# Two more slice pairs of each head pair as seven products of quarters, with work moved from VectorE to ScalarE

## The chip, the cores and the metric

The kernel runs on one core of one Trainium2 chip, as one launch. The metric is the device time of the whole program in microseconds (us), the median of several runs. All arithmetic is float32.

## The reference, cut to what matters

Two model blocks follow each other over 256 tokens of width 1024. The first projects the normed input with one wide matrix, and feeds four branches of 8 heads: a state-space scan (a), a block attention (b), a forgetting attention (c) and a sliding-window attention (d). The change lies in that projection.

```python
proj = h @ w_in
(m_z, m_xbc, m_dt, b_qkv, c_qkv, c_f, d_q, d_kv, gate_logits) = jnp.split(proj, SPLIT_POINTS, axis=-1)
y_a = mamba2_branch(m_z, m_xbc, m_dt, ...)          # x and z of the state: parts of m_xbc and m_z
y_b = moba_attention(heads(bq), heads(bk), heads(bv), ...)
y_c = forgetting_attention(heads(cq), heads(ck), heads(cv), c_f + forget_bias)
y_d = sliding_window_attention(heads(d_q), heads(dk), heads(dv), ...)
branch_out = jnp.einsum('bsiw,iwd->bsid', branches, w_branch)
gates = jax.nn.sigmoid(gate_logits)
x = x + jnp.sum(gates * branch_out, axis=2) @ w_out
```

## The kernel before, in words

The program is written out by hand for each engine: an engine runs its own list of instructions in order, and a step waits on counters of the steps that it needs. What is named `steps` in the code (`pe.step("g5734.0.1")`) is such a count. Nothing is reordered by a scheduler.

The first block does its heads in four **head pairs** (`pe_heads`, `act_heads`, `dve_heads`, `sp_heads`, i = 0 to 3). Each pair takes 17 slices of the wide matrix, each 128 columns by 1024 rows, loaded by SyncE into twelve 512 KB `slots`: q, k and v of b and c (BQ, BK, BV, CQ, CK, CV), q of d (DQ), the state's x and z (XS, ZS), and eight gate slices. A slice's product with the 256 tokens is plain (`project`: 8 matmuls of 128x256), or two slices together are done as **seven products of quarters**: tokens halved, rows halved, the two slices as the two column halves, seven products of four 128x128 matmuls (`quarter_product`) in place of eight. For this VectorE first makes sums of the weight quarters (s3, s1, s2, s4: four operations on 128x512, s1 in place in the slot), and afterwards puts the results together (a first sum, and three others, L2018 and L2025 to L2029 for gates). In the kernel before the gates (`gate_pair`, four a pair) and q and k of b and of c (`qk_pair`, in pairs 1 to 3) go this way; the values of b and c (L677, one matmul over two slices) and x and z (L491) are plain.

The order on TensorE in a pair: q/k of b, of c, q of d, the scores (L569), the values, x, z, the turning of the first head's softmax weights (L575 to L577), gate_pair(0), the turning of x (L700, L701) and of the second head's weights, gate_pair(1), the weighing of the values (L595, L597), gate_pair(2), and in pair 3 a sum of squares (`ya.sum`), gate_pair(3).

VectorE interleaves with this the maxima of the scores (L1954), the softmax weights (L1967), the convolution of x (L1869, L1873, L1876), the sums for the gates (`slice_sums`, L2006 to L2012; `first_sums`; `other_sums`), and `ada(0)` to `ada(5)` (L1983), six steps a pair that gather a modulation for the second block from 512 KB loads into two buffers.

SyncE issues all loads of a pair in one order, and waits before each until its buffer is free. The part that matters here, for pair i:

```python
ada_load(2)
...
ada_load(3)      # waits for ada(1)
gate_load(3)
...              # BV and CV of pair i + 1, gate_load(6)
ada_load(4)      # waits for ada(2): two buffers
gate_load(7)
decay_loads(i + 1)
gate_load(4)     # slots 9 and 10, free when gate_pair(0) is done
gate_load(5)
ada_load(5)      # waits for ada(3)
```

gate_load(4) and gate_load(5) bring the slices of gate_pair(2), gate_load(2) and gate_load(3) those of gate_pair(1). `decay_loads` are two broadcast loads of 384 and 256 KB, not there in pair 3.

Of the kernel before, what the change touches and what calls it, by code (L numbers as in the profile page):

```python
# [147 lines left out]
def build(nc, a, out):  # L148

    with ExitStack() as ctx:  # L150
# [106 lines left out]
        vs = carve(TT, 2 * P)  # L257
# [6 lines left out]
        xsT = carve(T)  # L264
        xdt = carve(TT, P)
        zs = carve(T)
# [151 lines left out]
        S["d1"] = bank[1][:, T:T + P], bank[0][:, T:]  # L418
# [3 lines left out]
        QK_SLOTS = {"b": (BQ, BK), "c": (CQ, CK)}  # L422
# [32 lines left out]
        def qk_banks(i):  # L455

            return [view3(bank[(i + n) % 2][:, :], P) for n in range(2)]
# [121 lines left out]
        def weigh_two(e, i, one, two):  # L579

            def parts(what, hh):
                if what == "y":
                    return xdt[:, 0, hh * HD:hh * HD + HD], xdt[:, 1, hh * HD:hh * HD + HD], dec[hh]
                if what == "d":
                    g = hh * HD
                    return dv[:, 0, g:g + HD], dv[:, 1, g:g + HD], PT[hh][2]
                at = "bc".index(what) * P + hh * HD
                return vs[:, 0, at:at + HD], vs[:, 1, at:at + HD], PT[hh]["bc".index(what)]
# [11 lines left out]
        def pe_heads(e, i):  # L600
            def gate_pair(n):
# [24 lines left out]
            def qk_pair(b):  # L626

                even, odd = QK_SLOTS[b]
                one, two = qk_banks(i)
                s2, s3, s4 = gate_sums(i - 1, "bc".index(b))  # L630
                low, high = hT[:, 0:4, :], hT[:, 4:8, :]
                e.wait_ge(*in_slot[even].upto(f"w{even}.{i}"))
                e.wait_ge(*dve.upto(f"gc11.3.{i - 1}" if b == "b" else f"qk11.b.{i}"))
                quarter_product(e, one[:, 0, :], slot[even][:, 0:512], low[:, :, tokens(0)])
                quarter_product(e, one[:, 1, :], slot[even][:, 512:], high[:, :, tokens(0)])
                e.wait_ge(*dve.upto(f"qs2.{b}.{i}"))
                quarter_product(e, one[:, 2, :], s2, xt[1]).then_inc(*pe.step(f"q126.{b}.{i}"))
                e.wait_ge(*dve.upto(f"gc1221.3.{i - 1}" if b == "b" else f"qk1221.b.{i}"))
                e.wait_ge(*dve.upto(f"qs4.{b}.{i}"))
                quarter_product(e, two[:, 0, :], slot[odd][:, 0:512], xt[0])  # L640
                quarter_product(e, two[:, 1, :], s3, xt[2])
                quarter_product(e, two[:, 2, :], s4, high[:, :, tokens(1)])
                quarter_product(e, two[:, 3, :], slot[odd][:, 512:], xt[3]).then_inc(*pe.step(f"q5734.{b}.{i}"))

            if i:
                qk_pair("b")
                qk_pair("c")
# [22 lines left out]
            e.wait_ge(*dve.upto(f"qd.{i}"))  # L670
            scores(e, "d", i).then_inc(*pe.step(f"s.d.{i}"))

            e.wait_ge(*in_slot[BV].upto(f"w{BV}.{i}"))
            e.wait_ge(*in_slot[CV].upto(f"w{CV}.{i}"))
# [6 lines left out]
            e.wait_ge(*in_slot[XS].upto(f"w{XS}.{i}"))  # L681
            e.wait_ge(*dve.upto(f"mx.d11.{i}"))
            project(e, part(i, 5), slot[XS], hT).then_inc(*pe.step(f"xs.{i}"))
            e.wait_ge(*in_slot[ZS].upto(f"w{ZS}.{i}"))
            project(e, part(i, 6), slot[ZS], hT).then_inc(*pe.step(f"zs.{i}"))

            e.wait_ge(*dve.upto(f"v.{i}"))
# [14 lines left out]
            e.wait_ge(*dve.upto(f"p.b1.1.{i}"))  # L702
            e.wait_ge(*act.upto(f"pt.b0.{i}"))
            turn_weights(e, "b", 1).then_inc(*pe.step(f"t.b1.{i}"))
            e.wait_ge(*dve.upto(f"p.c1.1.{i}"))
            e.wait_ge(*dve.upto(f"pt.c0.{i}"))
            turn_weights(e, "c", 1).then_inc(*pe.step(f"t.c1.{i}"))
            e.wait_ge(*dve.upto(f"p.d1.1.{i}"))
# [5 lines left out]
            e.wait_ge(*dve.upto(f"pt.c1.{i}"))  # L714
# [143 lines left out]
        def quarter_product(e, out, w, rhs):  # L858
            for k in range(4):
                end = e.matmul(out, w[:, k * P:(k + 1) * P], rhs[:, k, :], start=k == 0, stop=k == 3)  # L860
            return end
# [618 lines left out]
        def act_heads(e, i):  # L1480
# [9 lines left out]

            def exps(b):
# [27 lines left out]
            for b in "bcd":  # L1519
                exps(b)  # L1520
            e.wait_ge(*pe.upto(f"xs.{i}"))
            e.wait_ge(*dve.upto(f"xs.tap3.{i - 1}" if i else "bc3.tap3"))
            e.activation(pad1[:, CONV1 - 1:], part(i, 5), ACT.Copy).then_inc(*act.step(f"xpad.{i}"))
            e.wait_ge(*pe.upto(f"zs.{i}"))
            if i:
                e.wait_ge(*dve.upto(f"zs.{i - 1}"))
            e.activation(zt, part(i, 6), ACT.Tanh, scale=0.5).then_inc(*act.step(f"zt.{i}"))
            e.wait_ge(*dve.upto(f"xs.tap3.{i}"))
            e.activation(th[:, :], conv[:, :], ACT.Tanh).then_inc(*act.step(f"xs.tanh.{i}"))
            turned("b", 0)  # L1530
            turned("d", 0)
# [5 lines left out]
            turned("b", 1)  # L1537
            turned("d", 1)
# [393 lines left out]
        def dve_heads(e, i):  # L1932
# [25 lines left out]
            def weights(hh):  # L1958
# [3 lines left out]
                e.wait_ge(*dve.upto(f"r.{hh}.{i}"))  # L1962
                for n, b in enumerate("bcd"):
                    for t in range(TT):
                        at, m = (0, P) if t == 0 else (P + 1, T)
                        w = Lg[hh][:, n, at:at + m]
                        e.tensor_scalar(w, w, sm[:, 6 * hh + 2 * n + t:6 * hh + 2 * n + t + 1], None,  # L1967
                                        ALU.mult).then_inc(*dve.step(f"p.{b}{hh}.{t}.{i}"))

            def turned(hh):  # L1970
                e.wait_ge(*pe.upto(f"t.c{hh}.{i}"))
                if i:
                    e.wait_ge(*pe.upto(f"pv.c0b1.{i - 1}"))
                e.tensor_copy(PT[hh][1], TURN["c"][:, 0:3 * P]).then_inc(*dve.step(f"pt.c{hh}.{i}"))
# [19 lines left out]
            def slice_sums(n):  # L1994

                even, odd = GATE_SLOTS[n]
                s2, s3, s4 = gate_sums(i, n)
# [5 lines left out]
                elif i:  # L2003
                    e.wait_ge(*pe.upto(f"q5734.c.{i}"))
                    e.wait_ge(*dve.upto(f"mx.d11.{i - 1}"))
# [25 lines left out]
            def qk_sums(b, i):  # L2031

                even, odd = QK_SLOTS[b]
                s2, s3, s4 = gate_sums(i - 1, "bc".index(b))
# [3 lines left out]
                e.wait_ge(*pe.upto(f"g5734.{2 if b == 'b' else 3}.{i - 1}"))  # L2038
# [8 lines left out]
            def qk_first(b):  # L2047

                q = qk[b]
                e.wait_ge(*act.upto(f"qp1.{b}.{i}"))  # L2050
                e.tensor_tensor(q[:, 0:4:3, :], q[:, 1:2, :].to_broadcast([P, 2, P]), qk_banks(i)[0][:, 1:3, :],
                                ALU.add).then_inc(*dve.step(f"qk11.{b}.{i}"))

            def qk_other(b):

                q, two = qk[b], qk_banks(i)[1]
# [8 lines left out]
            if i:  # L2065
                qk_sums("c", i)
                qk_first("b")
                ada(0)
                qk_other("b")
# [1360 lines left out]
```

## Time and profile before

| what | value |
|---|---|
| median of 3 runs | 1058.26 us (1057.3 to 1058.48) |
| the profiled execution | 1057.9 us |
| its span, first to last instruction | 1055.9 us |
| TensorE busy | 1045.8 us (99%) |
| VectorE busy | 754.8 us (71%) |
| ScalarE busy | 237.4 us (22%) |
| moved by DMA | 162.67 MB, mean 154 GB/s |

The span is shorter than the profiled execution by what lies before the first and after the last instruction. A float32 matmul stands in the trace as two records, so a quarter product is 8 records and seven of them 56. A busy TensorE is an engine with a matmul in flight.

### The profile page before, as it was taken

What the parts mean: (1) busy time and instruction counts of PE and PEld (TensorE: products, weight loads), DVE (VectorE), ACT (ScalarE), POOL (GpSimd) and SP (SyncE); (2) the same over time, 40 slices, a digit from 0 to 9 for tenths busy, and PEclk for the clock granted to TensorE, in tenths of its full rate; (3) what the DMA queues carried; (4) which work ended last, traced back from release to release, by engine and by line L of the source; (5) the groups of instructions that cost most, each with busy time, mean ns of one, the idle gap of its engine ahead of it and who ended that gap; (6) DMA issues with size and microseconds to landing.
All of it is one profiled execution on the core that took longest, in us unless ns stands there. A gap on an engine that the chain in (4) does not pass through costs nothing.

```text
span 1055.9 us, 21666 instructions
## 1 busy us (share of the span) xinstructions
PE 1045.8 (99%) x8902; PEld 904.3 (86%) x8902; DVE 754.8 (71%) x1714; ACT 237.4 (22%) x630; POOL 121.0 (11%) x166
## 2 busy tenths in 40 slices
PE   9999999999999999999999999999999999999997
PEld 8899899998988499999644988898898989887983
DVE  4488776867743477777757788767878778777875
ACT  4032222213300120011101432323223232324101
POOL 1101000000045121100250000000000000000052
PEclk9999999999999999999999999999999999999999
DMA  8786666552377446554555333333333322161261
GB/s 271 260 308 234 208 197 220 194 186 86 120 228 230 159 71 251 195 190 162 182 194 220 99 102 101 99 103 101 105 102 97 120 82 80 42 241 41 81 160 40
DMA packets 72307, 162.67 MB, mean 154 GB/s; under 512 B 18929, under 2 KB 33169, under 8 KB 72210
## 3 DMA queue, kind: packets, MB, share of 16 engines
q1 hardware_dynamic: 71202, 159.67, 46.1%
q8 instruction: 71, 1.16, 0.4%
q10 hardware_dynamic: 1008, 1.63, 0.4%
q14 instruction: 26, 0.21, 0.1%
HBM read 160.17 MB, written 1.11 MB: 153 GB/s over the span
## 4 chain that ended last, share of the span: by engine, by line
PE 97%; DVE 1%; DMA 1%; issue 0%; ACT 0%; POOL 0%; DVEq 0%; ACTq 0%; POOLq 0%
PE bank L860 27%; PE bank L1015 18%; PE bank L491 13%; PE bank L926 6%; PE bank L1041 4%; PE bank L677 3%; PE bank L792 2%; PE bank L835 2%; PE bank L1186 2%; PE bank L1198 2%; PE bank L1355 2%; PE bank L988 1%; PE bank L1077 1%; PE bank L994 1%; PE bank L569 1%; PE bank L1055 1%
## 5 line engine op out<-in xcount | busy, mean ns | idle before, releaser
L1015 PE MATMUL bank<-hT,slots 128*128 128x256 f32 x896 | 204.5, 382 | 0.0
L1015 PEld LDWEIGHTS bank<-hT,slots 128*128 128x128 f32 x896 | 167.8, 190 | 23.2 <-issue 0.3
L860 PE MATMUL bank<-hT,slots 128*128 128x128 f32 x832 | 103.5, 276 | 0.0
L2511 DVE SCALAR_TENSOR_TENSOR arena<-padA,par,arena 128x256 f32<-128x256 f32 x232 | 102.8, 504 | 0.0
L860 PEld LDWEIGHTS bank<-hT,slots 128*128 128x128 f32 x832 | 97.9, 192 | 0.8 <-issue 0.7
L860 PE MATMUL bank<-arena,slots 128*128 128x128 f32 x768 | 95.6, 275 | 0.0
L860 PEld LDWEIGHTS bank<-arena,slots 128*128 128x128 f32 x768 | 90.9, 192 | 0.5
L491 PE MATMUL bank<-hT,slots 128*128 128x256 f32 x336 | 74.4, 380 | 0.0
L491 PEld LDWEIGHTS bank<-hT,slots 128*128 128x128 f32 x336 | 63.4, 190 | 9.2 <-issue 0.8
L491 PE MATMUL bank<-arena,slots 128*128 128x256 f32 x304 | 66.3, 380 | 0.5 <-DMA slots<-in_w_br 0.5
L491 PEld LDWEIGHTS bank<-arena,slots 128*128 128x128 f32 x304 | 57.5, 190 | 8.8 <-DMA slots<-in_w_br 1.1
L926 PE MATMUL bank<-slots,arena 128*128 128x512 f32 x128 | 55.4, 592 | 0.0
L926 PEld LDWEIGHTS bank<-slots,arena 128*128 128x128 f32 x128 | 24.2, 190 | 30.1 <-issue 25.6
L3052 POOL TENSOR_TENSOR arena<-arena 128x256 f32<-128x256 f32 x8 | 5.8, 728 | 359.8 <-ACT arena L1726 359.8
L860 PE MATMUL bank<-x,arena 128*128 128x128 f32 x352 | 46.5, 275 | 0.0
L860 PE MATMUL bank<-x,slots 128*128 128x128 f32 x352 | 46.5, 275 | 0.0
L860 PEld LDWEIGHTS bank<-x,slots 128*128 128x128 f32 x352 | 42.8, 192 | 0.0
L860 PEld LDWEIGHTS bank<-x,arena 128*128 128x128 f32 x352 | 42.8, 192 | 0.0
L1983 DVE SCALAR_TENSOR_TENSOR adaA<-arena,sc,adaA 128x1024 f32<-128x1024 f32 x24 | 30.7, 1277 | 0.0
L1595 ACT ACTIVATE arena<-bank 128x128 f32<-128x128 f32 x20 | 5.5, 277 | 110.2 <-PE bank L860 98.9
L2981 POOL TENSOR_TENSOR arena<-arena 128x256 f32<-128x256 f32 x8 | 8.0, 1020 | 188.8 <-DMA arena<-cum_scratch 188.8
L2168 DVE SCALAR_TENSOR_TENSOR arena<-arena,bank 128x256 f32<-128x256 f32 x32 | 12.6, 415 | 22.9 <-PE bank L491 15.8
(478 smaller groups left out, 1887.5 us busy)
## 6 DMA issues: line engine op xcount, KB each, us to landing
slots<-in_w_rwkv SPq DMA_DIRECT2D x72, 512.0 KB, 3.6
slots<-in_w_heads SPq DMA_DIRECT2D x64, 512.0 KB, 4.5
slots<-in_w_gu SPq DMA_DIRECT2D x44, 512.0 KB, 4.5
arena<-in_ada_w SPq DMA_DIRECT2D x24, 512.0 KB, 5.5
slots<-in_w_down SPq DMA_DIRECT2D x20, 512.0 KB, 4.4
slots<-in_w_br SPq DMA_DIRECT2D x32, 256.0 KB, 2.8
slots<-in_w_out SPq DMA_DIRECT2D x16, 512.0 KB, 4.2
slots<-in_w_y SPq DMA_DIRECT2D x16, 512.0 KB, 6.5
```

The source lines that it names most:

```text
L491: end = e.matmul(psum, w[:, k * P:(k + 1) * P], rhs[:, k, :], start=k == 0, stop=k == kt - 1)
L677: end = e.matmul(view3(bank[5][:, t * T:(t + 1) * T], P), hT[:, k, t * P:(t + 1) * P], slots[:, BV:CV + 1, k * P:(k + 1) * P], start=k == ...
L792: return e.matmul(bank[DOWN_BANK[m]][:, :], *sides, start=j == 0, stop=j == OUT_PAIRS - 1)
L835: end = e.matmul(psum[:, tokens(t)], w[:, k * P:(k + 1) * P], hT[:, k, tokens(t)], start=k == 0, stop=k == KT - 1)
L860: end = e.matmul(out, w[:, k * P:(k + 1) * P], rhs[:, k, :], start=k == 0, stop=k == 3)
L926: return e.matmul(bank[DOWN_BANK[m]][:, :], *sides, start=j == 0, stop=j == DOWN - 1)
L1015: end = e.matmul(proj(w, q), slot[w][:, k * P:(k + 1) * P], hT[:, k, :], start=k == 0, stop=k == KT - 1)
L1041: end = e.matmul(out[:, at, :], w[:, k * P:(k + 1) * P], rhs[:, k, :], start=k == 0, stop=k == 3)
L1186: end = e.matmul(bank[2][r, c * CHUNK:(c + 1) * CHUNK], Nt[r, c, :], Xs[r, c, :], start=True, stop=True)
L1198: end = e.matmul(chunks(half(3))[r, c, :], Z[r, c, :], Gs[r, c, :], start=True, stop=True)
L1983: e.scalar_tensor_tensor(out=third, in0=adaW[n % 2], scalar=sc[:, 2 * i + n // 3:2 * i + n // 3 + 1], in1=third, op0=ALU.mult, op1=ALU.add ...
L2511: e.scalar_tensor_tensor(out=o, in0=src, scalar=w, in1=o, op0=ALU.mult, op1=ALU.add).then_inc(*dve.step(f"tap{n}.{q}"))
```

## The change

In every head pair the values of b with those of c (called "v"), and x with z ("z"), are done as seven products of quarters by `slice_pair`, which was `qk_pair`. For the values the roles in the matmul are turned (`quarter_product_turned`: tokens stand, weights move), since tokens are wanted on the rows. VectorE makes eight more weight sums a pair (`pair_weights`) and puts two more results together (`pair_first`, `pair_other`). The copy of the values out of PSUM falls away. The second head's softmax weights are scaled by ScalarE (`second_weights`), as are q of d; the turned weights of c are copied by ScalarE. The places of `slice_sums` and `ada` in VectorE's list move. SyncE's list keeps its order; the steps that its waits name change.

```diff
             def slice_pair(b):
+                even, odd = PAIR_SLOTS[b]
+                one, two = pair_banks(b, i)
+                s2, s3, s4 = pair_sums(b, i)
+                product = quarter_product_turned if b == "v" else quarter_product
...
+                elif b == "z":
+                    e.wait_ge(*dve.upto(f"qk11.v.{i}"))
+                product(e, one[:, 0, :], slot[even][:, 0:512], low[:, :, tokens(0)])
+                product(e, one[:, 1, :], slot[even][:, 512:], high[:, :, tokens(0)])
+                e.wait_ge(*dve.upto(f"qs2.{b}.{i}"))
+                product(e, one[:, 2, :], s2, xt[1]).then_inc(*pe.step(f"q126.{b}.{i}"))
...
+                product(e, two[:, 3, :], slot[odd][:, 512:], xt[3]).then_inc(*pe.step(f"q5734.{b}.{i}"))
@@ pe_heads
-            for t in range(TT):
-                for k in range(KT):
-                    end = e.matmul(view3(bank[5][:, t * T:(t + 1) * T], P), hT[:, k, t * P:(t + 1) * P],
-                                   slots[:, BV:CV + 1, k * P:(k + 1) * P], start=k == 0, stop=k == KT - 1)
-            end.then_inc(*pe.step(f"vbc.{i}"))
-            project(e, part(i, 5), slot[XS], hT).then_inc(*pe.step(f"xs.{i}"))
-            project(e, part(i, 6), slot[ZS], hT).then_inc(*pe.step(f"zs.{i}"))
+            slice_pair("v")
+            slice_pair("z")
@@ act_heads
+            def second_weights():
+                e.wait_ge(*dve.upto(f"r.1.{i}"))
+                for n, b in enumerate("bcd"):
+                    for t in range(TT):
...
+                        e.activation(w, w, ACT.Copy, scale=sm[:, 6 + 2 * n + t:6 + 2 * n + t + 1]).then_inc(*act.step(f"p.{b}1.{t}.{i}"))
...
+            exps("b")
+            exps("c")
+            pair_product("v")
+            exps("d")
+            second_weights()
...
+            pair_product("z")
+            e.wait_ge(*dve.upto(f"qk1221.z.{i}"))
+            e.activation(pad1[:, CONV1 - 1:], xsT, ACT.Copy).then_inc(*act.step(f"xpad.{i}"))
+            e.activation(zt, zs, ACT.Tanh, scale=0.5).then_inc(*act.step(f"zt.{i}"))
+            turned("b", 0)
+            turned("c", 0)
+            turned("d", 0)
             e.wait_ge(*dve.upto(f"xs.tap3.{i}"))
             e.activation(th[:, :], conv[:, :], ACT.Tanh).then_inc(*act.step(f"xs.tanh.{i}"))
@@ dve_heads
             for b in "bcd":
                 maxima(b)
+            pair_first("v")
             decays(0)
             decays(1)
-            slice_sums(1 if i else 0)
-            if i == 0:
-                ada(0)
-            e.tensor_copy(vs, view3(bank[5][:, :], T)).then_inc(*dve.step(f"v.{i}"))
-            weights(0)
-            ada(2 if i else 1)
+            pair_other("v")
+            inverses(0)
+            first_weights()
+            inverses(1)
+            slice_sums(0)
+            pair_first("z")
             if i == 0:
                 ada(0)
+            pair_other("z")
             conv_silu(e, ("xs", f".{i}"), act.upto(f"xpad.{i}"), i * CONV1, 8 * CONV1 + i, xsT)
...
-            weights(1)
-            turned(0)
             if i == 0:
-                ada(2)
-                slice_sums(1)
+                ada(1)
             first_sums(0)
-            ada(3)
+            slice_sums(1)
             other_sums(0)
+            ada(2)
             e.wait_ge(*pe.upto(f"turn.x.{i}"))
...
-            turned(1)
-            ada(4)
+            ada(3)
             first_sums(1)
             slice_sums(2)
             other_sums(1)
+            ada(4)
             slice_sums(3)
```

**How it moves instructions.** TensorE, head pair 1, from the last score matmul on; L677 is the values, L491 x and z:

```order
L569 MATMUL bank0<-arena 128x256
L677 MATMUL bank5<-slots,hT 128x256 x16
L491 MATMUL bank1<-hT,slots 128x256 x8
L491 MATMUL bank0<-hT,slots 128x256 x8
L575 MATMUL bank5<-cst,arena 128x128
```

The same place in the changed kernel; L870 is the turned quarter product, L865 the other, L580 the first turning of weights:

```order
L574 MATMUL bank5<-arena 128x256
L870 MATMUL bank1<-slots,hT 128x128 x8
L870 MATMUL bank1<-arena,x 128x128 x4
L870 MATMUL bank0<-slots,x 128x128 x4
L870 MATMUL bank0<-arena,x 128x128 x4
L870 MATMUL bank0<-arena,hT 128x128 x4
L870 MATMUL bank0<-slots,x 128x128 x4
L865 MATMUL bank1<-hT,slots 128x128 x8
L865 MATMUL bank1<-x,arena 128x128 x4
L865 MATMUL bank0<-x,slots 128x128 x4
L580 MATMUL bank5<-cst,arena 128x128
```

Thirty-two matmuls of 128x256 have become 56 of 128x128.

VectorE, head pair 1, before, from `ada(2)` (the first L1983) to `other_sums(0)`; L1869 to L1876 are the convolution, L1974 the copy of turned weights, L2018 `first_sums(0)`:

```order
L1983 SCALAR_TENSOR_TENSOR adaA<-arena,sc,adaA 128x1024
L1869 TENSOR_SCALAR conv<-padA,arena 128x256
L1873 SCALAR_TENSOR_TENSOR conv<-padA,arena,conv 128x256 x3
L1876 SCALAR_TENSOR_TENSOR arena<-th,conv 128x256
L2096 SCALAR_TENSOR_TENSOR arena<-arena,bank1 128x256
...
L1974 COPY arena<-bank2 128x384
L2018 TENSOR_TENSOR arena<-arena,bank0 128x2x128
L1983 SCALAR_TENSOR_TENSOR adaA<-arena,sc,adaA 128x1024
L2025 TENSOR_TENSOR arena<-arena,bank1 128x256
```

The same stretch in the changed kernel; L1905 ends the convolution, L2043 is `first_sums(0)`, L2031 to L2037 `slice_sums(1)`, L2050 to L2054 `other_sums(0)`, L2007 `ada(2)`:

```order
L1905 SCALAR_TENSOR_TENSOR arena<-th,conv 128x256
L2126 SCALAR_TENSOR_TENSOR arena<-arena 128x256
L2043 TENSOR_TENSOR arena<-arena,bank0 128x2x128
L2031 TENSOR_TENSOR arena<-slots 128x512
L2033 TENSOR_TENSOR slots<-slots 128x512
L2035 TENSOR_TENSOR arena<-slots 128x512
L2037 TENSOR_TENSOR arena<-slots,arena 128x512
L2050 TENSOR_TENSOR arena<-arena,bank1 128x256
L2052 TENSOR_TENSOR arena<-arena,bank1 128x128
L2054 TENSOR_TENSOR arena<-arena,bank1 128x256
L2007 SCALAR_TENSOR_TENSOR adaA<-arena,sc,adaA 128x1024
```

`ada(2)`, which stood ahead of the convolution, now stands behind `slice_sums(1)` and `other_sums(0)`.

## Rows read from the trace of the kernel before

**Rows 1.** The waits of TensorE over the whole span: us, times, longest.

```profile
PE bank L522 <- POOL padA L2972: 1.2, 1, 1.2
...
PE bank L491 <- DMA slots<-in_w_br: 0.5, 1, 0.5
```

**Rows 2.** The chain that ended last, in time: start us, us, what; start, pairs 0, 1.

```profile
1.16 7.53 PE bank L522 x24
...
55.24 7.10 PE bank L677 x32
...
115.52 2.17 PE bank L569 x24
117.68 7.10 PE bank L677 x32
124.78 6.91 PE bank L491 x32
...
132.68 6.25 PE bank L860 x56
...
140.13 6.25 PE bank L860 x56
...
149.13 25.21 PE bank L860 x224
```

**Rows 3.** Timeline of VectorE in pair 1: start us, us, line, operation.

```profile
126.76 1.47 DVE L1967 TENSOR_SCALAR arena<-arena 128x128 f32<-128x128 f32 x6
128.14 1.27 DVE L1983 SCALAR_TENSOR_TENSOR adaA<-arena,sc,adaA 128x1024 f32<-128x1024 f32 x1
129.34 0.41 DVE L1869 TENSOR_SCALAR conv<-padA,arena 128x256 f32<-128x256 f32 x1
129.78 1.52 DVE L1873 SCALAR_TENSOR_TENSOR conv<-padA,arena,conv 128x256 f32<-128x256 f32 x3
132.45 0.42 DVE L1876 SCALAR_TENSOR_TENSOR arena<-th,conv 128x256 f32<-128x256 f32 x1 [1.15 <-ACT th L1529]
...
143.86 0.69 DVE L2006 TENSOR_TENSOR arena<-slots 128x512 f32<-128x512 f32 x1
...
146.65 0.41 DVE L2025 TENSOR_TENSOR arena<-arena,bank 128x256 f32<-128x256 f32 x1
...
147.76 0.68 DVE L2006 TENSOR_TENSOR arena<-slots 128x512 f32<-128x512 f32 x1
...
150.54 0.47 DVE L2120 SCALAR_TENSOR_TENSOR arena<-arena,par,bank 128x256 f32<-128x256 f32 x1
```

**Rows 4.** Timeline of ScalarE in pair 1.

```profile
107.07 0.42 ACT L1515 ACTIVATE arena<-arena 128x256 f32<-128x256 f32 x1 [4.53 <-DVE arena L2063]
```

**Rows 5.** Timeline of SyncE's issues in pair 1: ada 4, gates 4 and 5.

```profile
129.45 0.33 SPq L3134 DMA_DIRECT2D arena<-in_ada_w  x1
...
138.96 0.82 SPq L3101 DMA_DIRECT2D slots<-in_w_heads  x2
```

**Rows 6.** Timeline of SyncE's issues in pair 0: ada 4, and gates 4 and 5.

```profile
74.05 0.33 SPq L3134 DMA_DIRECT2D arena<-in_ada_w  x1
...
76.51 0.82 SPq L3101 DMA_DIRECT2D slots<-in_w_heads  x2
```

**Rows 7.** Issues of line L3134 from 74 to 74.3 us: time to landing.

```profile
DMA to landing us min/median/max: 3.7/3.7/3.7
```

**Rows 8.** Issues of line L3101 from 76.4 to 77.5 us: who waited, time to landing.

```profile
L3101 SPq DMA_DIRECT2D slots<-in_w_heads x2: 340/389/438, 76.5 to 76.9; - x2
...
  DVE arena L2006: 1.8, 1
...
DMA to landing us min/median/max: 7.1/7.6/8.0
```

**Rows 9.** Stretches of the span: us, PE, PEld, DVE, ACT, POOL busy, PEclk, DMA, GB/s.

```profile
100.00:160.00 60.00, 60.00 (x474) 56.32 (x474) 46.48 (x114) 15.12 (x49) 1.66 (x4) 1.00 0.62 207
...
1050.00:1056.00 6.00, 0.00 (x0) 0.00 (x0) 2.67 (x8) 1.53 (x6) 0.00 (x0) 0.78 0.47 175
```

More of the change, by code:

```diff
@@ L263, in build @@
         cm = carve(2, 3 * P)
-        xsT = carve(T)
+        xz = carve(4, P)
+        xsT, zs = (xz[:, n:n + 2, :].rearrange("p a b -> p (a b)") for n in (0, 2))
         xdt = carve(TT, P)
-        zs = carve(T)
         zt = carve(T)
@@ L453, in gate_sums, with pair_banks, pair_sums @@
             return [v.rearrange("p a b -> p (a b)") for v in free[3 * (n % 2):3 * (n % 2) + 3]]
-        def qk_banks(i):
-            return [view3(bank[(i + n) % 2][:, :], P) for n in range(2)]
+        def pair_banks(b, i):
+            return [view3(bank[(i + n + (b in "vz")) % 2][:, :], P) for n in range(2)]
+        def pair_sums(b, i):
+            return gate_sums(max(i - 1, 0), b in "bv")
         def gate_rows(i, n):
@@ L639, in qk_pair @@
                 e.wait_ge(*dve.upto(f"qs4.{b}.{i}"))
[L640 to L643, printed above, removed]
+                product(e, two[:, 0, :], slot[odd][:, 0:512], xt[0])
+                product(e, two[:, 1, :], s3, xt[2])
@@ L645, in pe_heads @@
+                product(e, two[:, 2, :], s4, high[:, :, tokens(1)])
+                product(e, two[:, 3, :], slot[odd][:, 512:], xt[3]).then_inc(*pe.step(f"q5734.{b}.{i}"))
             if i:
-                qk_pair("b")
-                qk_pair("c")
+                slice_pair("b")
+                slice_pair("c")
             else:
@@ L860, in quarter_product, with quarter_product_turned @@
                 end = e.matmul(out, w[:, k * P:(k + 1) * P], rhs[:, k, :], start=k == 0, stop=k == 3)
+            return end
+        def quarter_product_turned(e, out, w, lhs):
+            for k in range(4):
+                end = e.matmul(out, lhs[:, k, :], w[:, k * P:(k + 1) * P], start=k == 0, stop=k == 3)
             return end
@@ L1537, in act_heads @@
             turned("b", 1)
+            turned("c", 1)
             turned("d", 1)
@@ L1956, in maxima, with inverses @@
                                                accum_out=mx[:, k:k + 1]).then_inc(*dve.step(f"mx.{b}{hh}{t}.{i}"))
-            def weights(hh):
+            def inverses(hh):
                 e.wait_ge(*act.upto(f"e.d{hh}.1.{i}"))
@@ L1965, in weights @@
                         at, m = (0, P) if t == 0 else (P + 1, T)
[L1966 to L1974, printed above, removed]
+                        w = Lg[0][:, n, at:at + m]
+                        e.tensor_scalar(w, w, sm[:, 2 * n + t:2 * n + t + 1], None, ALU.mult).then_inc(*dve.step(f"p.{b}0.{t}.{i}"))
             def ada(n):
@@ L2065, in dve_heads @@
             if i:
-                qk_sums("c", i)
-                qk_first("b")
+                pair_weights("c", i)
+                pair_first("b")
                 ada(0)
-                qk_other("b")
-                qk_first("c")
+                pair_other("b")
+                pair_weights("v", i)
+                pair_first("c")
                 ada(1)
-                qk_other("c")
-                queries("d", 4)
-                slice_sums(0)
+                pair_other("c")
+                pair_weights("z", i)
             else:
```

122 lines of the change are left out of this document (61 added, 61 removed).

## The prediction, made before the changed kernel was run

> **What bounds the kernel now.** I read TensorE's waits first. There are three in the whole span, the longest 1.2 us at the start [rows 1], so TensorE's own list sets the end, and each us taken from it is a us, as long as no wait opens. The chain of waits then gives the pieces of a head pair [rows 2]. From the scores' end (call it S, 117.68 in pair 1) TensorE runs the values 7.10 us, x and z 6.91, nine turnings (131.69 to 132.68) 0.99, gate_pair(0) 6.25, eleven turnings (138.93 to 140.13) 1.20, gate_pair(1) 6.25, the weighing (146.38 to 149.13) 2.75, then gate pairs 2 and 3. Third, since a shorter list only helps if the others keep up, I read VectorE's and SyncE's timelines around gate_pair(2) [rows 3, 5, 6]. In pair 1 its two slices are issued at 138.96, the moment gate_pair(0) ends and frees their slots [rows 5]. VectorE begins their sums at 143.86, and needs 2.18 us to the third [rows 3], while TensorE reaches the product that uses it at 149.13 plus two products: some 4.9 us in hand. In pair 0 the same two loads take 7.1 and 8.0 us, and VectorE waited 1.8 us for them [rows 8]. That is the thin place.
>
> **What TensorE saves.** Seven products of quarters, four matmuls each, take 6.25 us [rows 2], so 0.893 each. The values lose 7.10 - 6.25 = 0.85 us and x with z 6.91 - 6.25 = 0.66, together 1.51 a pair and 6.04 in four. The turned product for the values has the same shape as the other; I cost it the same. Bounds: no dearer, or dearer by what the values' plain product is over x and z, 7.10 - 6.91 = 0.19 a pair.
>
> **What is added and moved, and its cover.** VectorE gets two more sets of weight sums a pair (143.86 to 146.65, so 2.79 each) and two results (the other sums 146.65 to 147.76, 1.11, and the first sum about 0.35); it loses the second head's weights (126.76 to 128.14, 1.38), the copy of the values and two copies of turned weights. VectorE is busy 46.5 of 60 us in this stage [rows 9], so as work this fits; its order decides. ScalarE's six scalings have no row: an ACTIVATE of 128x256 is 0.42 us [rows 4], six at most 2.5, at least about 1.4 as on VectorE. They are done while VectorE makes slice_sums(0), 2.79 long, so I cost them at nothing; without that cover first_sums of z would wait, at most 2.5 us, with about 1.1 in hand before gate_pair(0).
>
> Now VectorE's list, counted from S. TensorE ends v at S+6.25, z at S+12.50, the turnings at 13.49, gate_pair(0) at 19.74; call that E. VectorE: the rest of v by 7.6, the inverse, six weights and the next inverse 9.1, slice_sums(0) 11.9, first sum of z 12.3; z's last product is seen at 12.7, the others by 13.8; ScalarE's copy of x 14.2, the convolution's taps (129.34 to 131.26) 16.1, tanh, the two products behind it and ScalarE's copy for the first sum some 1.9, so first_sums(0) by 18.0; slice_sums(1) 20.8, other_sums(0) 21.9, and only then **ada(2)** (128.14 to 129.34, 1.20) at 23.1 or 23.2: **E + 3.45**. Before, ada(2) ended at 129.34, over 9 us ahead of the end of gate_pair(0) at 138.93.
>
> **Who waits for ada(2).** SyncE's ada_load(4) goes when ada(2) has freed its buffer, 129.45 in pair 1 [rows 3, 5]. Its queue is in order, so gate_load(7), the two decay loads and, last, gate_load(4) and gate_load(5) stand behind that wait. Pair 0 before shows what the six cost in a row [rows 6 to 8]: ada 4 is issued at 74.05 and lands 3.7 later; gates 4 and 5 are issued at 76.5 and 76.9 and land at 83.6 and 84.9, so 9.55 and 10.85 us after ada 4. Bounds for this: all six at the pace of the last two, 1.3 us per 512 KB, would be 2.4 + 5.25 x 1.3 = 9.2 us; the upper end is 1.5 us over what is shown, for other loads in flight. I take 10.85, since it is the same six loads.
>
> **A middle pair (1 and 2), counted from E.** Gate 4 lands at 3.45 + 9.55 = 13.0, gate 5 at 14.3. Without a stall gate_pair(2) starts at 1.20 + 6.25 + 2.75 = 10.2. It waits 2.8 us for its first slice; after two products (14.8) it waits for the third sum (14.3 + 2.18 = 16.5), 1.7; a product later (17.4) it waits until VectorE has put gate_pair(1) together, which stands behind slice_sums(2) (14.3 + 2.79 + 1.11 = 18.2), 0.8; it ends at 21.8. gate_pair(3) waits for the first sum of gate_pair(2), behind ada(4), slice_sums(3) (2.79), the two products with the state's y (about 0.9) and itself: 23.5, so 1.7. Sum 7.0 us, less 1.51.
>
> **Pair 0.** ada(0) now delays z's sums and ada(1) stands behind the convolution: ada(1) ends at S+19.2, after SyncE's ada_load(3) and, behind it, gate_load(3), have waited for it. Gate 3 lands 3.7 + 1.3 later, S+24.3; its third sum is there at 26.5, and gate_pair(1) wants it at 22.7: 3.8, then 0.8 for other_sums(0), so gate_pair(1) ends at 31.8. ada(2) ends at 29.4, gates 4 and 5 land at 39.0 and 40.3, gate_pair(2) wanted the first at 34.5: 4.4, then 1.7, 0.8 and 1.7 as above. Sum 13.2.
>
> **Pair 3.** No decay loads, so gate 5 lands at E + 3.45 + 3.7 + 3 x 1.3 = 11.05: third sum 13.2 against 12.0 wanted, 1.25, then 0.8. The sum of squares waits for VectorE (14.95, ada(4) 1.2, 2.79, 0.9, a 1024-wide product 1.2: 21.0) against 18.5: 2.5. Sum 4.55.
>
> **The sum.** 13.2 + 2 x 7.0 + 4.55 = 31.75 us of waits less 6.04 is 25.7. On the profiled execution, 1057.9 us (0.4 below the median of the runs shown), that is 1083.6; I say **1083**, slower by 2.4%.
>
> **A rule weighed.** TensorE's granted clock is 1.00 all through the heads, and 0.78 over the last 6 us, which begin after its last matmul [rows 9]: an idle engine falls from the 2.4 to the 1.2 GHz level. The sum takes it that stalls up to 4.4 us long leave the clock where it is. The Trainium skill, "TensorE: Matmul & The Clock Gate", section "Part 1: The HAM clock gate (the "warmup" mystery)", says that the throttled clock is the default and that only sustained activity releases it; by that rule the longer of these stalls could each be followed by slow matmuls, and the sum would be that of the third rival. No row here shows a stall in the middle of the program, so it stays open.
>
> **The rivals.**
> 1. **The covers hold: faster.** If gate 5 landed by E+9.8, its third sum would be there by 12.0, when gate_pair(2) wants it; TensorE would then gain its 6.04 and the time be 1052. From the end of ada(2) at E+3.45 that leaves 6.35 us for the six loads, which take 10.85 [rows 6 to 8], or, with those as shown, ada(2) done before E-1. For it: in pair 1 gates 4 and 5 had 4.9 us in hand. Against: VectorE's chain from z's last product to ada(2) holds no idle time to win 4.5 us from. 5%.
> 2. **Stalls, but shorter: 1074.** The loads at the pace of their best, 9.2 us, take 1.65 off each of three pairs, 4.95; ada(2) a us earlier in all four, because VectorE and ScalarE overlap better than I add up, takes 4 more: 1083 - 9 = 1074. If gate_pair(3) also finds its sum ready (1.7 in three pairs), 1069. 22%.
> 3. **The clock falls in the stalls: 1090.** At the start 24 records of 128x256 took 7.53 us [rows 2] where 32 take 6.91 later, so 24 take 5.18: 2.35 us lost to a slow start. One such loss for the longest stall of pairs 0, 1 and 2 is 7 us more. 14%.
> 4. **It does less than it says: no change.** If the waits shrank to about 1.5 us a pair they would just eat the saving. 2%.
>
> **How the numbers follow.** The forecast has the remaining 57%, with its own range 1077 to 1088. A measurement here tells 0.2%, 2.1 us, from no change. Every case but the first and the fourth is slower by more: 0.93 slower, 0.02 the same, 0.05 faster. The range that should hold the time 8 times in 10 takes in most of the second and third rivals and the loads' bounds: 1068 to 1092.
>
> **What would show it.** Right: TensorE's waits, absent before, at the first matmul of gate_pair(2) on the slots, and inside it and at gate_pair(3) on VectorE; ada_load(4) issued some 3.5 us after gate_pair(0) ends, gates 4 and 5 right behind it; the 56 records of v and of z in 6.25 us each; pair 0 losing about twice as much as pair 1. Wrong: gates 4 and 5 landing within 10 us of E; matmul records of over 300 ns after a stall (rival 3); v slower than z (the turned form); a wait at gate_pair(0), which would make ScalarE's scalings or z's sums the cause.

## The result, and the profile after

| kernel | median us | lowest to highest | ratio to before, 95% interval |
|---|---|---|---|
| before, four runs beside it | 1057.78 | 1056.96 to 1058.48 | |
| changed | 1088.47 | 1088.13 to 1089.32 | 1.0288 [1.0276, 1.0300] |

Slower by 30.7 us, where 25 to 26 were forecast. TensorE's waits over the whole span come first, because they decide (us in all, times, longest):

```profile
PE bank L865 <- DMA slots<-in_w_heads: 8.9, 4, 3.5
PE bank L865 <- DVE arena L2035: 7.5, 4, 5.2
PE bank L865 <- DVE arena L2043: 4.2, 3, 1.4
PE bank L865 <- DVE arena L2054: 2.4, 4, 0.7
```

Before, the longest wait in the whole span was the 1.2 us at the start [rows 1]. Now there are 23 us of waits on one line, L865, the line of every quarter product. What was waited for says where: the slot of a gate slice (4, one a pair), the third sum of a slice (L2035, in `slice_sums`), the first result of a gate pair (L2043, in `first_sums`) and the last of the others (L2054, in `other_sums`). TensorE's share of the span fell from 99 to 97%, and it was busy for 1052.5 us where it had been for 1045.8, although its products had become cheaper. Part of its work ran at a lower clock; e4 below is about that.

```profile
PE 1052.5 (97%) x9094; PEld 914.8 (84%) x9094; DVE 774.1 (71%) x1738; ACT 251.8 (23%) x674; POOL 119.0 (11%) x166
```

The chain in pair 1 (start us, us, what) is the counterpart of [rows 2]. The two changed products have become 6.45 and 6.27 us of 56 records each, seven quarter products in both. (The order shown with the change leaves out the last three of x and z.) Then the chain leaves TensorE, and at 156.11 it hangs on a load.

```profile
128.72 2.17 PE bank L574 x24
130.89 6.45 PE bank L870 x56
137.34 6.27 PE bank L865 x56
...
156.11 8.01 DMA slots<-in_w_heads
```

S, the end of the scores, is 130.89 here. VectorE's timeline (start us, us, operation; in brackets the idle time before it) shows ada(2), the SCALAR_TENSOR_TENSOR of 1024 columns, from 152.99 to 154.27, where [rows 3] had it at 128.14, beside the first product of x. Before its next slice sum it then stands idle for 8.37 us, until the slices of gate_pair(2) are there:

```profile
152.99 1.28 DVE L2007 SCALAR_TENSOR_TENSOR adaA<-arena,sc,adaA 128x1024 f32<-128x1024 f32 x1
...
165.86 0.69 DVE L2031 TENSOR_TENSOR arena<-slots 128x512 f32<-128x512 f32 x1 [8.37 <-issue]
```

SyncE's issues, to be held against [rows 5], are one tight row behind it: ada 4, gate 7, the two decay loads, gates 4 and 5. The last two took 8.0 and 9.1 us to land, and they are what VectorE's slice sum waited for (8.4 us in their own view).

```profile
154.29 0.33 SPq L3162 DMA_DIRECT2D arena<-in_ada_w  x1
154.66 0.44 SPq L3129 DMA_DIRECT2D slots<-in_w_heads  x1
155.20 0.38 SPq L3183 DMA_DIRECT2D arena<-cum_scratch  x1
155.62 0.43 SPq L3184 DMA_DIRECT2D arena<-cum_scratch  x1
156.11 1.05 SPq L3129 DMA_DIRECT2D slots<-in_w_heads  x2
```

```profile
  DVE arena L2031: 8.4, 1
...
DMA to landing us min/median/max: 8.0/8.5/9.1
```

And TensorE's timeline, gate_pair(2) of pair 1 and, at 175.14, the start of gate_pair(3). The brackets are the waits forecast, in their order: the slot, the third sum, the other results, the first result.

```profile
164.17 3.38 PE L865 MATMUL bank<-hT,slots 128*128 128x128 f32 x16 [3.14 <-DMA slots<-in_w_heads]
168.06 1.16 PE L865 MATMUL bank<-x,arena 128*128 128x128 f32 x8 [0.51 <-DVE arena L2035]
169.89 1.16 PE L865 MATMUL bank<-x,slots 128*128 128x128 f32 x8 [0.68 <-DVE arena L2054]
...
175.14 2.02 PE L865 MATMUL bank<-hT,slots 128*128 128x128 f32 x16 [1.41 <-DVE arena L2043]
```

### The profile page after: what moved, and what is told of

Same layout as the page of the kernel before. It is cut to its first block, busy times and chain, and to the rows that moved or that the text cites. A ratio compares the mean times of both kernels' runs of the same rounds, so it can differ in the third digit from the quotient of the medians.

```text
span 1086.5 us, 22127 instructions
## 1 busy us (share of the span) xinstructions
PE 1052.5 (97%) x9094; PEld 914.8 (84%) x9094; DVE 774.1 (71%) x1738; ACT 251.8 (23%) x674; POOL 119.0 (11%) x166
## 4 chain that ended last, share of the span: by engine, by line
PE 86%; DVE 6%; DMA 4%; issue 3%; ACT 1%; SPq 0%; DVEq 0%; ACTq 0%
PE bank L865 23%; PE bank L1025 18%; PE bank L496 9%; PE bank L936 6%; PE bank L1051 4%; DMA slots<-in_w_heads 3%; PE bank L870 2%; PE bank L797 2%; PE bank L840 2%; PE bank L1196 2%; PE bank L1208 2%; PE bank L1365 2%; PE bank L998 1%; PE bank L1087 1%; DMA slots<-in_w_br 1%
## 5 line engine op out<-in xcount | busy, mean ns | idle before, releaser
L1025 PE MATMUL bank<-hT,slots 128*128 128x256 f32 x896 | 204.5, 382 | 0.0
L1025 PEld LDWEIGHTS bank<-hT,slots 128*128 128x128 f32 x896 | 167.8, 190 | 23.2 <-issue 0.3
L865 PE MATMUL bank<-hT,slots 128*128 128x128 f32 x896 | 115.3, 282 | 13.1 <-DMA slots<-in_w_heads 8.9
L865 PEld LDWEIGHTS bank<-hT,slots 128*128 128x128 f32 x896 | 109.0, 197 | 14.6 <-DMA slots<-in_w_heads 9.9
L865 PE MATMUL bank<-arena,slots 128*128 128x128 f32 x768 | 95.6, 275 | 0.0
L865 PEld LDWEIGHTS bank<-arena,slots 128*128 128x128 f32 x768 | 90.9, 192 | 0.5
L865 PE MATMUL bank<-x,arena 128*128 128x128 f32 x416 | 58.3, 286 | 7.6 <-DVE arena L2035 7.5
L865 PEld LDWEIGHTS bank<-x,arena 128*128 128x128 f32 x416 | 53.4, 201 | 8.8 <-DVE arena L2035 8.8
L865 PE MATMUL bank<-x,slots 128*128 128x128 f32 x416 | 57.2, 282 | 2.4 <-DVE arena L2054 2.4
L865 PEld LDWEIGHTS bank<-x,slots 128*128 128x128 f32 x416 | 52.2, 197 | 3.2 <-DVE arena L2054 3.2
L496 PE MATMUL bank<-hT,slots 128*128 128x256 f32 x208 | 46.1, 380 | 0.0
L3080 POOL TENSOR_TENSOR arena<-arena 128x256 f32<-128x256 f32 x8 | 5.8, 728 | 359.8 <-ACT arena L1755 359.8
L496 PEld LDWEIGHTS bank<-hT,slots 128*128 128x128 f32 x208 | 39.0, 190 | 5.9 <-issue 0.8
L1499 ACT ACTIVATE arena<-arena 128x512 f32<-128x512 f32 x16 | 10.1, 631 | 118.7 <-DVE arena L2054 118.7
L2031 DVE TENSOR_TENSOR arena<-slots 128x512 f32<-128x512 f32 x16 | 10.9, 679 | 35.4 <-issue 35.4
L2007 DVE SCALAR_TENSOR_TENSOR adaA<-arena,sc,adaA 128x1024 f32<-128x1024 f32 x24 | 30.7, 1278 | 0.0
```

Of the source, the lines that this page charges most:

```text
L496: end = e.matmul(psum, w[:, k * P:(k + 1) * P], rhs[:, k, :], start=k == 0, stop=k == kt - 1)
L1025: end = e.matmul(proj(w, q), slot[w][:, k * P:(k + 1) * P], hT[:, k, :], start=k == 0, stop=k == KT - 1)
L2007: e.scalar_tensor_tensor(out=third, in0=adaW[n % 2], scalar=sc[:, 2 * i + n // 3:2 * i + n // 3 + 1], in1=third, op0=ALU.mult, op1=ALU.add ...
```

## The experiments

The theory on trial: the whole loss is that ada(2), and in pair 0 ada(0) and ada(1), come late in VectorE's list, so that SyncE's in-order list, which holds the loads of the gates behind them, is late too. Its rivals: the clock falls in the stalls and that is what costs; VectorE has too much to do, whatever its order; the new products themselves are no gain.

In all nine kernels the length of each head pair, from the start of its values' product to the start of the next pair's (pair 3: to the first product of the mix of the branches, which follows the heads), comes from the chains, so from one traced execution of each:

| kernel | pair 0 | pair 1 | pair 2 | pair 3 | median us | ratio to before |
|---|---|---|---|---|---|---|
| before | 62.44 | 62.28 | 62.28 | 45.88 | 1058.25, 1057.96 | |
| changed | 75.77 | 68.87 | 68.89 | 50.19 | 1088.47 | 1.0288 [1.0276, 1.0300] |
| e3, before with ada(2) late | 62.52 | 69.26 | 68.98 | 52.69 | 1076.75 | 1.0178 [1.0161, 1.0196] |
| e2, ada(2) early in pairs 1 to 3 | 76.13 | 60.97 | 60.97 | 44.58 | 1067.86 | 1.0093 [1.0078, 1.0108] |
| e1, loads ahead of the wait | 65.48 | 60.98 | 60.97 | 44.88 | 1057.19 | 0.9990 [0.9981, 1.0000] |
| e7, gate 3 ahead of ada 3 | 71.88 | 69.58 | 68.52 | 50.70 | 1085.08 | 1.0258 [1.0242, 1.0274] |
| e4, the stalls filled | 76.49 | 68.56 | 68.34 | 52.00 | 1090.11 | 1.0302 [1.0285, 1.0320] |
| e6, ada(0) to ada(2) early | 62.43 | 60.97 | 60.97 | 44.57 | 1053.96 | 0.9963 [0.9950, 0.9975] |
| e5, e1 with ada(0), ada(1) early | 62.07 | 60.97 | 60.97 | 44.88 | 1053.50 | 0.9964 [0.9951, 0.9976] |

(The two medians of before belong to the two groups of runs: e1 to e4, and e5 to e7.)

**The cause alone, in the kernel before (e3).** No product is changed; in pairs 1 to 3 ada(2) moves to where the change has it, behind other_sums(0), and ada(3) and ada(4) follow later too.

```diff
             weights(0)
-            ada(2 if i else 1)
+            if i == 0:
+                ada(1)
...
             first_sums(0)
-            ada(3)
+            if i == 0:
+                ada(3)
             other_sums(0)
+            if i:
+                ada(2)
...
             turned(1)
-            ada(4)
+            if i:
+                ada(3)
+            else:
+                ada(4)
...
             other_sums(1)
+            if i:
+                ada(4)
```

> The kernel before, without any new product of quarters, with ada(2) alone moved behind other_sums(0) in pairs 1 to 3 (ada(3) and ada(4) follow one place later). Queue theory: this one move makes gate_pair(2) wait as in the changed kernel, 6 to 7 us in pairs 1 and 2, 3 to 5 in pair 3: 1072 to 1078 us. Rival (the new products and sums are needed for the loss): 1058 to 1061.

Measured: 1076.75 us, 18.5 above the kernel before. Pair 0, which it leaves alone, stayed at 62.5; pairs 1 and 2 rose by 7.0 and 6.7, pair 3 by 6.8. (The four runs spread from 1075.53 to 1079.25, and the traced one took 1077.91, so the pairs add up to more than the median shows.) TensorE's waits show the same set of places as the changed kernel's (L2010, L2018 and L2029 are there the third sum, the first result and the last one, L501 is the sum of squares in pair 3):

```profile
PE bank L860 <- DMA slots<-in_w_heads: 5.1, 2, 2.6
PE bank L860 <- DVE arena L2018: 2.8, 2, 1.4
PE bank L860 <- DVE arena L2010: 2.8, 2, 1.5
PE bank L501 <- DVE arena L2135: 2.2, 1, 2.2
PE bank L860 <- DVE arena L2029: 2.0, 3, 0.7
```

Pair 3 was expected to lose 3 to 5 us. Behind the wait of 2.2 us its sum of squares took 3.58 us where it took 1.73 before, with the granted clock at 0.85 and 0.81 around it (295 to 300, 300 to 305), and nothing behind it had to be waited for:

```profile
298.68 3.58 PE bank L501 x8
```

Those 1.85 us are what pair 3 lost beyond the 5. So the places of these 1.2 us steps alone, with not a product or a byte changed, cost some 7 us a pair.

**The same one step, undone in the changed kernel (e2).**

```diff
             decays(1)
+            if i:
+                ada(2)
             pair_other("v")
...
             other_sums(0)
-            ada(2)
+            if i == 0:
+                ada(2)
```

> The changed kernel with ada(2) of pairs 1 to 3 moved ahead of the other sums of the values; SyncE's order, pair 0 and all else as changed. Queue theory: pairs 1 to 3 lose their waits (6.6, 6.6 and 4.3 us over before turn into 1.3 saved each), pair 0 keeps its 13.3: 1066 to 1069 us. Rival (VectorE is simply too full in these pairs): the same work in another order, so no more than 4 us better, 1084 or above.

Measured: 1067.86. Pairs 1 and 2 are 60.97, which is 1.31 shorter than before the change, and pair 3 is 1.30 shorter. The products pay off as soon as nothing waits. All that is left of the loss is pair 0:

```profile
PE bank L865 <- DVE arena L2035: 7.2, 2, 5.7
PE bank L865 <- DMA slots<-in_w_heads: 3.0, 1, 3.0
```

**The queue instead of the step (e1).** VectorE's list stays as changed; in SyncE's, gate loads 3, 6 and 7 go ahead of ada_load(3), and 4 and 5 ahead of ada_load(4). Gates 4 and 5 still stand behind ada_load(3), which waits for ada(1).

```diff
-            ada_load(3)
             gate_load(3)
...
             gate_load(6)
-            ada_load(4)
             gate_load(7)
+            ada_load(3)
+            gate_load(4)
+            gate_load(5)
+            ada_load(4)
             if more:
...
                 decay_loads(i + 1)
-            gate_load(4)
-            gate_load(5)
             ada_load(5)
```

> The changed kernel with SyncE's order alone altered: the gate slices ahead of the ada loads, the decay loads behind them. Queue theory (gates 4 and 5 stand behind ada_load(4), which waits for ada(2)): the waits of gate pairs 2 and 3 go in pairs 1 to 3, some 2 us are left in pair 0, the time is 1053 to 1056 us, faster than before. Rival (VectorE's added sums and their order are what TensorE waits for): VectorE's list is untouched, so the waits stay and the time is above 1075.

Measured: 1057.19, a little above what was expected. ada(2) of pair 1 is as late as in the changed kernel (142.89 to 144.17, 3.4 us after gate_pair(0)), and yet pairs 1 and 2 are 60.98 and 60.97, as with ada(2) early. It was never ada(2)'s own result that TensorE missed; it was the loads queued behind the wait for it. What was missed is pair 0: 65.48, some 4.4 us over a pair 0 without waits (61.1, worked out below), where 2 were expected. SyncE's timeline shows gates 4 and 5 issued in time, at 75.4, as gate_pair(0) ends:

```profile
69.00 0.33 SPq L3162 DMA_DIRECT2D arena<-in_ada_w  x1
69.37 3.60 SPq L3129 DMA_DIRECT2D slots<-in_w_heads  x7
75.00 0.33 SPq L3162 DMA_DIRECT2D arena<-in_ada_w  x1
75.37 0.91 SPq L3129 DMA_DIRECT2D slots<-in_w_heads  x2
```

But the row begins at 69.00 with ada_load(2), which waits for ada(0), late in pair 0, and eight loads lie right behind it, ahead of gates 4 and 5. In this stretch the DMA engines are full,

```profile
70.00:86.00 16.00, 14.60 (x132) 13.81 (x133) 12.55 (x25) 5.20 (x14) 0.00 (x0) 1.00 0.99 388
```

and gates 4 and 5 land 10.1 and 10.9 us after they were issued. It is the same wait one step further up; in e5 below, where ada(0) is early, the row begins at 61.98.

**One load past one wait (e7).** Only `gate_load(3)` goes ahead of `ada_load(3)`.

```diff
-            ada_load(3)
             gate_load(3)
+            ada_load(3)
```

> The changed kernel with gate_load(3) alone put ahead of ada_load(3) in SyncE's list. Queue theory: in pair 0 the wait of 5.2 us in gate_pair(1) shrinks to under 1, pairs 1 to 3 stay (their ada(1) is early): 1083 to 1086 us, 3 to 5 below the changed kernel's 1088.5. Rival (pair 0's loss sits in gate_pair(2), which waits longer by what gate_pair(1) saves): 1087 or above.

Measured: 1085.08, 3.4 us less than the changed kernel, 3.9 of it in pair 0. In the changed kernel gate_pair(1) of pair 0 waits for its third sum like this (TensorE's timeline):

```profile
83.27 2.08 PE L865 MATMUL bank<-x,arena 128*128 128x128 f32 x8 [5.21 <-DVE arena L2035]
```

and in e7 like this:

```profile
80.06 1.16 PE L865 MATMUL bank<-x,arena 128*128 128x128 f32 x8 [1.31 <-DVE arena L2035]
```

The wait shrank by 3.9 us, though not to under 1 as expected. So of what pair 0 lost 3.9 us hung on gate 3 standing behind the wait for ada(1).

**The clock (e4).** In the changed kernel the clock does fall. Stretches of pair 1 (us; busy PE, PEld (TensorE's weight loads), DVE, ACT, POOL; PEclk, the granted clock; DMA share; GB/s):

```profile
160.00:165.00 5.00, 1.86 (x20) 1.48 (x17) 0.00 (x0) 0.00 (x0) 1.65 (x4) 0.97 0.97 351
165.00:170.00 5.00, 3.81 (x21) 3.33 (x21) 3.97 (x8) 0.13 (x1) 0.00 (x0) 0.69 0.93 242
170.00:175.00 5.00, 3.73 (x32) 3.54 (x32) 4.86 (x9) 2.08 (x6) 0.00 (x0) 1.00 0.47 118
```

Behind the wait of 3.14 us, the granted clock is 0.69 from 165 to 170, part of that stretch at 1.2 GHz in place of 2.4. The first two products of gate_pair(2) take 3.38 us, against 1.95 for the first two of x and z in the same pair. Does that cost? e4 puts matmuls that nobody reads into the waits of pairs 0 to 2, so that the engine stays busy; it leaves nothing of the computation out.

```diff
+                def fill(count, b):
+                    for _ in range(count):
+                        e.matmul(half(b), hT[:, 0, 0:P], hT[:, 0, :], start=True, stop=True)
+
+                if n == 2 and i < PAIRS - 1:
+                    fill(7 if i else 9, 2)
                 e.wait_ge(*in_slot[even].upto(f"wg{2 * n}.{i}"))
...
                 quarter_product(e, one[:, 1, :], slot[even][:, 512:], high[:, :, tokens(0)])
+                if n == 2 and i < PAIRS - 1:
+                    fill(3, 2)
+                if n == 1 and i == 0:
+                    fill(10, 7)
                 e.wait_ge(*dve.upto(f"gs2.{n}.{i}"))
```

> The changed kernel with matmuls that nobody reads put into TensorE's stalls of pairs 0 to 2 (10 ahead of the third product of gate_pair(1) in pair 0; 9, 7 and 7 ahead of gate_pair(2), 3 ahead of its third product). Clock theory: the granted clock stays 1.00, the slow stretches behind the stalls go, and the time falls by 2 to 6 us, to 1082 to 1086, though work was added. Rival (the clock costs nothing, since the slow stretch only fills the next wait): 1088 or above, with the later waits longer.

Measured: 1090.11, no gain. The clock was held, as the same stretches of e4 show:

```profile
160.00:165.00 5.00, 5.00 (x38) 3.81 (x34) 0.00 (x0) 0.00 (x0) 1.65 (x4) 1.00 1.03 349
165.00:170.00 5.00, 4.55 (x31) 3.81 (x30) 3.46 (x7) 0.00 (x0) 0.00 (x0) 1.00 0.99 265
```

yet pairs 1 and 2 won only 0.3 and 0.55 us. The slow products ran while the next thing they needed, the third sum, was not there either: where they ran slowly the wait for it was 0.51 us, less than the 1.7 forecast at full clock. Pair 3, which e4 does not fill, tells the same from the other side. In the changed kernel the clock falls inside gate_pair(2), two of its products take 2.03 and 1.86 us, and the sum of squares then waits 0.62 (TensorE's timeline):

```profile
304.51 2.03 PE L865 MATMUL bank<-x,slots 128*128 128x128 f32 x8 [0.68 <-DVE arena L2054]
306.33 1.86 PE L865 MATMUL bank<-x,arena 128*128 128x128 f32 x8
...
310.60 1.99 PE L506 MATMUL bank<-arena,cst 128*128 128x256 f32 x8 [0.62 <-DVE arena L2154]
```

In e4 those products run at full clock, and the sum of squares starts at practically the same time, after a wait of 2.25:

```profile
304.63 1.16 PE L876 MATMUL bank<-x,slots 128*128 128x128 f32 x8 [0.68 <-DVE arena L2065]
305.62 1.06 PE L876 MATMUL bank<-x,arena 128*128 128x128 f32 x8
...
310.72 2.49 PE L506 MATMUL bank<-arena,cst 128*128 128x256 f32 x8 [2.25 <-DVE arena L2165]
```

Behind that wait its clock falls too (0.71 from 310 to 315), and there gate_pair(3) finds all it needs, so the loss stays: 7.40 us (from the chain) in place of 6.25.

```profile
313.20 7.40 PE bank L876 x56
```

That is most of the 1.8 us by which e4's pair 3 is longer than the changed kernel's. In pair 0 the clock of the changed kernel falls furthest, to 0.54 from 85 to 90 us, and is 1.00 there in e4; yet e4's pair 0 is 0.7 longer. gate_pair(2) started there at 96.50 rather than 95.67, still behind a wait for its slot. Why the load came later was not tried.

**The step moved everywhere, the queue left alone (e6).** In VectorE's list only, against the changed kernel:

```diff
             decays(1)
+            if i:
+                ada(2)
+            else:
+                ada(0)
+                ada(1)
             pair_other("v")
...
             pair_first("z")
-            if i == 0:
-                ada(0)
             pair_other("z")
+            if i == 0:
+                ada(2)
...
-            if i == 0:
-                ada(1)
             first_sums(0)
...
             other_sums(0)
-            ada(2)
```

> The changed kernel with SyncE's order as it was changed, and only ada moved in VectorE's list: ada(2) of pairs 1 to 3, and ada(0) and ada(1) of pair 0, ahead of the other sums of the values, ada(2) of pair 0 ahead of the convolution. Queue theory: the place of ada alone made the loss, so the time is that of e5, 1052.5 to 1054.5 us, with VectorE's work unchanged in amount. Rival (SyncE's order has to change as well): 1060 or above.

Measured: 1053.96, faster than both kernels. SyncE's timeline in pair 1 looks like [rows 5] again: ada 4 goes early, and gates 4 and 5 go seven us later, the moment gate_pair(0) ends,

```profile
130.80 0.43 SPq L3164 DMA_DIRECT2D arena<-in_ada_w  x1
...
137.67 0.81 SPq L3131 DMA_DIRECT2D slots<-in_w_heads  x2
```

and these two land in half the time that they took in the row of six:

```profile
DMA to landing us min/median/max: 3.7/4.2/4.6
```

**Both orders (e5).** e1's order of the loads, and ada(0) and ada(1) of pair 0 early as in e6:

```diff
             decays(1)
+            if i == 0:
+                ada(0)
+                ada(1)
             pair_other("v")
...
             pair_first("z")
-            if i == 0:
-                ada(0)
...
-            if i == 0:
-                ada(1)
             first_sums(0)
```

> SyncE's order of e1_loads_first, and in pair 0 ada(0) and ada(1) moved into VectorE's idle time ahead of the other sums of the values. Queue theory: what e1 has left in pair 0 (4.4 us of waits behind late ada(0) and ada(1)) goes too, TensorE waits nowhere in the heads and the whole saving shows, 0.65 us for the values and 0.66 for x and z in each of four pairs: 1052.5 to 1054 us. Rival (pair 0 is held by its first loads, whatever VectorE does): as e1, 1057.

Measured: 1053.50, 4.5 us (0.36%) below the kernel before, not to be told from e6 by their intervals. All of TensorE's waits are these:

```profile
PE bank L527 <- POOL padA L2999: 1.2, 1, 1.2
PE bank L1051 <- DVE arena L2620: 0.7, 1, 0.7
PE bank L865 <- DVE arena L2043: 0.6, 1, 0.6
PE bank L501 <- ACT arena L1462: 0.3, 1, 0.3
```

And VectorE is busier in the heads than in the kernel before, 51.4 of 60 us against the 46.5 of [rows 9], while TensorE does not stop for it:

```profile
100.00:160.00 60.00, 60.00 (x534) 58.02 (x533) 51.43 (x119) 18.71 (x60) 2.12 (x4) 1.00 0.64 213
```

So the amount of VectorE's work was not the cause; its order was.

## Why the prediction was right, and where its sizes were off

**The mechanism and its place held.** TensorE's new waits are at the places named: the slot of gate_pair(2), its third sum, the other results, the first result of gate_pair(2) ahead of gate_pair(3). ada(2) ends 3.4 us after gate_pair(0) (154.27 against 150.84, which is S plus 19.95), and 3.45 was forecast. Gates 4 and 5 follow in SyncE's row as listed. Pair 0 loses twice what pair 1 does: 13.3 and 6.6 us net. e3 shows that the late steps alone do it, e2 that ada(2) early alone undoes it in pairs 1 to 3, e6 that ada(0) to ada(2) early undo all but 1.2 us of waits, and e1 that the in-order row of loads is what carries it. The time, 1088.47, lies inside the whole range and 0.5 us above the forecast's own, 1077 to 1088.

**The sum, term by term.** What the waits cost is told by the pairs of kernels without them. Pairs 1 and 2 are 60.97 in e6; pair 3 is 44.57; a pair 0 without waits is put at pair 1's plus the 0.16 by which it was longer before, 61.1. Against these the changed kernel's pairs are 14.7, 7.9, 7.9 and 5.6 longer, 36.1 in all; forecast were 13.2, 7.0, 7.0 and 4.55, 31.75. The products save 1.31 a pair, 5.24, not 6.04. 36.1 less 5.24 is 30.9, and 30.7 was measured. Not all of the 36.1 us is idle time: 23.6 stand as waits (23.0 on L865, 0.6 at the sum of squares in pair 3), and TensorE is busy for 11.6 us longer than in e6, 1052.5 against 1040.9.

- **The step that was short in the stalls: the loads' landing.** The six loads were costed as in pair 0 before, gate 4 landing 9.55 and gate 5 10.85 us after ada 4 was issued. In pair 1 it was 9.8 (164.1) and 11.5 (165.8). The first wait became 3.14 and not 2.8; and from the first product to the third it took 3.89 us (164.17 to 168.06) where two products take 1.79, so 2.1 went there and not 1.7. Together that is 0.7 of the 0.9 that a middle pair lost beyond the forecast. In pair 0, gate 3 was put at 5.0 us behind the issue of ada 3, and landed 6.2 behind it (75.19 plus 5.8, against 74.81); its wait, put at 3.8, reads 5.21. Behind that wait the rest of gate_pair(1) ran slowly, and the slot of gate_pair(2), forecast as a wait of 4.4, was waited for 1.86:

```profile
95.67 3.15 PE L865 MATMUL bank<-hT,slots 128*128 128x128 f32 x16 [1.86 <-DMA slots<-in_w_heads]
```

In pair 3 gate 5 was there 11.9 us after E, the end of gate_pair(0) (VectorE's first sum of it starts at 300.48, E being 288.58), not 11.05, which is most of the 1.1 by which that pair lost more than forecast.
- **The step that was wrong in the saving: the values.** They take 6.45 us, not 6.25, in every pair. The text had this as a bound (0.19 a pair), laid to the turned form. But the values cost 0.19 more than x and z before the change as well [rows 2], and the surcharge stayed: 7.10 to 6.45 is 0.65, as 6.91 to 6.27 is 0.64. The step that failed is taking the values down to 6.25 in spite of it. The turned form is not needed to explain it, though the plain product of the values had its tokens standing too: in the kernel before, gate_pair(2) of pair 3, which is not turned, also takes 6.45 us behind the weighing (from the chain),

```profile
273.69 6.45 PE bank L860 x56
```

and 25.21 us for the four in a row of [rows 2] is 0.21 more than four times 6.25. The values stand behind the scores, whose matmuls have 64 rows, and gate_pair(2) behind the weighing, whose matmuls have 64 columns. That this place is the cause is likely, but was not tried.
- **What was costed at nothing** (ScalarE's six scalings, behind slice_sums(0)) was nothing: no wait at gate_pair(0) in any pair.

**The rivals.** The first, that the covers hold, named its own condition: gate 5 landed by 9.8 us after gate_pair(0), with ada(2) early or with faster loads. e6 meets it with ada(2) early and e5 by the order of the loads, and they come to 1054.0 and 1053.5 where it said 1052; the 0.80 of the values and a wait of 0.6 to 1.2 us in pair 0 make up the difference. The second, shorter stalls, went the wrong way: loads and sums were later, not earlier. The third, the clock, had its premise right and its price wrong, though 1088.47 lies nearer to its 1090 than to the forecast's 1083. The clock fell in every pair, in stretches of 5 us to 0.54, 0.69, 0.79 and 0.70, and matmuls ran at the low level. The Trainium skill, "TensorE: Matmul & The Clock Gate", section "Part 1: The HAM clock gate (the "warmup" mystery)", says that an engine left idle is throttled and must be active to be released; the trace agrees. The 7 us that the rival added on top were not there: in e4 the clock was kept up through the filled waits, and the time did not fall. VectorE's and the loads' path set the start of the next piece, and the slow products ran inside that path's time. So the stalls were forecast as if the clock stayed up, it did not, and the sum hardly noticed. The prediction had no reason for that; it was luck.

Of the prediction's four signs of being wrong, two showed and two did not. Matmul records of over 300 ns did follow a stall (a median of 421 ns in the first two products of gate_pair(2) in pair 1, where 275 is the pace), and v was slower than z. Gates 4 and 5 did not land within 10 us of E (164.1 and 165.8 in pair 1, E being 150.84), and there was no wait at gate_pair(0).

## What to carry to other kernels

When a step is moved in one engine's list, look for every queue that waits for it, and read that queue down from the wait: a load that must wait in an in-order list holds back each load behind it, also those whose buffers have long been free. Steps of 1.2 us whose results TensorE did not wait for cost 7 to 8 us in a middle pair; moving them forward again turned 2.9% slower into 0.4% faster, and moving the needed loads ahead of the wait did so in all pairs but the first. And a product made cheaper pays only after the loads and sums of the next product have been placed anew, for it now asks for them earlier.

## What the runs showed of the hardware beyond expectation

- How long a 512 KB load took to land went with what was issued just ahead of it. Gates 4 and 5 of pair 1 landed 3.7 and 4.6 us after issue where ada 4 had gone seven us earlier (e6), 8.0 and 9.1 as the last of six in under 3 us (changed kernel), and those of pair 0 10.1 and 10.9 as the last of eleven in 7 us (e1).
- A fallen clock is not a loss by itself. The fall behind a stall of 3.14 us cost at most 0.3 us in pair 1 (68.87 against 68.56 in e4), because the next wait shrank; but 1.15 us behind a stall of 2.25 us in e4's pair 3, and 1.85 in e3's, where nothing was waited for next.
- A stall costs more than its bracket. In gate_pair(2) of pair 1, the starts of the third and the fourth product are 1.83 us apart (168.06, 169.89) where 0.89 is the pace without a wait; the third's row lasts 1.16, the bracket says 0.68, so 0.26 lies outside it.
